# Token attention in the order differential, neighbourhood, plain; two modulation parts in every step from the first step on

## What is computed

```python
for l in range(2):
    mod_x = silu(c) @ w_ada[l] + b_ada[l]              # six vectors of 1024: shifts, scales, gates
    hx = modulate(rms_norm(x, g1), sh1, sc1)           # the same for ctx
    q.. k.. v.. = split(hx @ w_in[l])                  # for three mixers
    # a, plain: 8 heads of 64, 2 key heads, softmax over 512 + 256 keys
    # b, neighbourhood: 4 heads of 64, a window of tokens (by a bias) + 256 context keys
    # c, differential: 4 heads, each two softmaxes of 32-wide halves
    w  = p[:, :, 0] - lam * p[:, :, 1]
    oc = rms_norm(w @ v, g_sub) * (1 - lam_init)       # normed per head, 64 wide
    x = x + gate1 * (concat([oa, ob, oc]) @ w_out[l])
    x = x + gate2 * conv_ffn(modulate(rms_norm(x, g2), sh2, sc2))
# then the second block: two layers of mixer, memory attention and feed-forward
```

## Time and profile before

| | before |
|---|---|
| median of three runs | 3666.6 us (3666.44 to 3673.21) |
| the profiled execution | 3661.56 us, span 3659.7 us |
| PE busy | 3528.0 us (96%) |
| DVE busy | 1755.0 us (48%) |
| ACT busy | 1524.8 us (42%) |
| POOL busy | 1458.4 us (40%) |
| mean granted TensorE clock | 0.985 |
| chain that ended last | PE 89%, DVE 5%, ACT 3% |

### The profile page before, as it was taken

The page is one execution under the profiler, slowest core; times in us unless marked ns, Lnnn a source line. Parts: engine busy times, 40 slices in busy tenths (PEclk is TensorE's granted clock), DMA queues, the critical chain, the costliest instruction groups (busy, mean ns, idle before and its releaser), DMA issues.

```text
span 3659.7 us, 50085 instructions
## 1 busy us (share of the span) xinstructions
PE 3528.0 (96%) x19796; PEld 2799.3 (76%) x19796; DVE 1755.0 (48%) x2922; ACT 1524.8 (42%) x2557; POOL 1458.4 (40%) x986
## 2 busy tenths in 40 slices
PE   7999889999999999899999989999999989999998
PEld 5776567888899766578887768878887768888886
DVE  5766645423334766633542776161114686162114
ACT  4445554433455446534332355443223355443222
POOL 4520014444588510034444435344444444434442
PEclk8999999999999999999999999999999999999999
DMA  7613513333365411423333213223333213323331
GB/s 230 161 48 115 174 35 93 93 98 96 105 185 173 114 45 42 155 87 101 93 98 96 76 34 104 81 73 95 97 94 81 75 41 87 98 61 101 93 98 58
DMA packets 642466, 355.59 MB, mean 97 GB/s; under 512 B 70469, under 2 KB 614841, under 8 KB 642233
## 3 DMA queue, kind: packets, MB, share of 16 engines
q1 hardware_dynamic: 630379, 339.66, 32.2%
q10 hardware_dynamic: 11854, 12.72, 1.1%
HBM read 346.28 MB, written 6.05 MB: 96 GB/s over the span
## 4 chain that ended last, share of the span: by engine, by line
PE 89%; DVE 5%; ACT 3%; issue 2%; DMA 1%; POOL 1%; SPq 0%; ACTq 0%; DVEq 0%
PE psum L876 67%; PE psum L1105 5%; PE psum L1136 3%; PE psum L1156 2%; PE psum L900 1%; DVE neg_max L2013 1%; PE psum L1077 1%; ACT work L1574 1%; PE psum L980 1%; PE psum L904 1%; PE psum L1185 1%; PE psum L1036 1%; PE psum L931 1%; PE psum L1163 1%; PE psum L1015 1%
## 5 line engine op out<-in xcount | busy, mean ns | idle before, releaser
L859 POOL TENSOR_TENSOR w_lo<-w_raw,w_hi 128x256 fp32r<-128x256 f32 (+3 forms) x936 | 1396.5, 1512 | 2126.3 <-ACT w_hi L1413 2126.0
L876 PE MATMUL psum<-h_hi,w_hi 128*128 128x512 f32 (+1 forms) x2736 | 1034.2, 378 | 2.5 <-POOL w_lo L859 1.5
L876 PE MATMUL psum<-h_lo,w_hi 128*128 128x512 f32 (+1 forms) x2736 | 1010.1, 369 | 0.0
L876 PE MATMUL psum<-h_hi,w_lo 128*128 128x512 f32 (+1 forms) x2736 | 1010.1, 369 | 0.0
L1413 ACT ACTIVATE w_hi<-w_raw 128x1024 fp32r<-128x1024 f32 (+1 forms) x546 | 570.9, 1047 | 622.5 <-PE psum L876 587.6
L876 PEld LDWEIGHTS psum<-h_hi,w_hi 128*128 128x128 f32 x2736 | 516.5, 189 | 112.0 <-issue 19.8
L876 PEld LDWEIGHTS psum<-h_lo,w_hi 128*128 128x128 f32 x2736 | 516.5, 189 | 94.7 <-issue 9.9
L876 PEld LDWEIGHTS psum<-h_hi,w_lo 128*128 128x128 f32 x2736 | 516.2, 189 | 87.4
L876 PE MATMUL psum<-hid_hi,w_hi 128*128 128x512 f32 (+1 forms) x1040 | 393.0, 378 | 1.8 <-POOL w_lo L859 1.7
L876 PE MATMUL psum<-hid_lo,w_hi 128*128 128x512 f32 (+1 forms) x1040 | 391.8, 377 | 0.0
L876 PE MATMUL psum<-hid_hi,w_lo 128*128 128x512 f32 (+1 forms) x1040 | 391.8, 377 | 0.0
(11 more groups left out here) (248 smaller groups left out, 4280.1 us busy)
## 6 DMA issues: line engine op xcount, KB each, us to landing
w_raw<-in_w_up_dram SPq DMA_DIRECT2D x132, 512.0 KB, 3.8
w_raw<-in_w_ff_dram SPq DMA_DIRECT2D x128, 512.0 KB, 3.8
w_raw<-in_w_in_dram SPq DMA_DIRECT2D x92, 512.0 KB, 3.9
w_raw<-in_w_ada_dram SPq DMA_DIRECT2D x80, 512.0 KB, 4.2
w_raw<-in_w_down_dram SPq DMA_DIRECT2D x48, 512.0 KB, 3.6
w_raw<-in_w_mkv_dram SPq DMA_DIRECT2D x32, 512.0 KB, 3.9
w_raw<-in_w_down_dram SPq DMA_DIRECT2D x24, 384.0 KB, 3.1
w_ada_first<-in_w_ada_dram SPq DMA_DIRECT2D x4, 2048.0 KB, 18.0
```

The lines of the kernel that those rows point to most:

```text
L859: m = nc.gpsimd.tensor_tensor(WL[:, c % NSPLIT, k:k + step, :], RAW[:, c % NRAW, k:k + step, :], WH[:, c % NSPLIT, k:k + step, :].bitcast( ...
L876: m = pe.matmul(out_ap, lhs(a, k), rhs(b, k), start=(k == 0 and n == 0), stop=(k == nk - 1 and n == 2))
```

## The change

For the 512 tokens the plan is now built in the order differential (steps 0 to 15), neighbourhood (16 to 23), plain (24 to 39); the context attention keeps its order. Tiles and their numbers stay. The modulation parts are counted from step 0: steps 0 to 23 in layer 0, steps 0 to 15 in layer 1. The rest of the differential norm moves into the loop: one square root and one reciprocal for both groups at std_at = 19, and the spread of the two groups at i = 20 and 21. lam_ends moves to i = 0. A plain or neighbourhood group now waits for the low part of the last such group before it, where before it was simply the group before.

```diff
-ADA_LAST = 36
...
-    pair = step - ADA_LAST + len(parts) // 2
-    return parts[2 * pair:2 * pair + 2] if pair >= 0 else []
+    return parts[2 * step:2 * step + 2]
...
+            def plain():
+                for m in range(4):
...
+            def window():
+                for j in range(2):
...
+            def differential():
+                for j in range(2):
...
+            if stream == "x":
+                differential()
+                window()
+                plain()
+            else:
+                plain()
+                window()
+                differential()
...
+        def std_at(att):
+
+            return max(i for i, o in att["ends"].items() if att["groups"][o]["diff"] is not None) + 4 if att["wide"] else None
+
         def spread_at(att, i):
 
-            diff = [o for o, g in enumerate(att["groups"]) if g["diff"] is not None]
-            return [o for n, o in enumerate(diff) if i == len(att["steps"]) + 2 * n]
+            if att["wide"]:
+                return [o for n, o in enumerate(diff_groups(att)) if i == std_at(att) + 1 + n]
+            return [o for n, o in enumerate(diff_groups(att)) if i == len(att["steps"]) + 2 * n]
...
-                        pe.wait_ge(*at("sub_rstd", (S, o)))
+                        pe.wait_ge(*at("sub_rstd", S if att["wide"] else (S, o)))
...
-                    for o in spread_at(att, i):
+                    if att["wide"] and i == std_at(att):
+                        act.wait_ge(*at("sub_taken", (S, groups[diff_groups(att)[-1]]["bank"])))
+                        nc.scalar.activation(SUBS[:, :, :], SUBS[:, :, :], ACT.Sqrt, bias=EPSC[:, 0:1],
+                                             scale=1.0 / HEAD).then_inc(*mark("sub_std", S))
+                    for o in () if att["wide"] else spread_at(att, i):
...
-                    if S == ("att", "x", 0) and i == 2:
+                    if S == ("att", "x", 0) and i == 0:
                         lam_ends()
...
-                        if o and g["diff"] is None:
-                            dve.wait_ge(*at("o_lo", (S, o - 1)))
+                        if g["diff"] is None and plain_before(att, o) is not None:
+                            dve.wait_ge(*at("o_lo", (S, plain_before(att, o))))
...
+                    if att["wide"] and i == std_at(att):
+                        dve.wait_ge(*at("sub_std", S))
+                        nc.vector.reciprocal(SUBS[:, :, :], SUBS[:, :, :]).then_inc(*mark("sub_rstd", S))
                     for o in spread_at(att, i):
-                        dve.wait_ge(*at("sub_std", (S, o)))
-                        nc.vector.reciprocal(sub_stats(att, o), sub_stats(att, o)).then_inc(*mark("sub_rstd", (S, o)))
+                        if not att["wide"]:
+                            dve.wait_ge(*at("sub_std", (S, o)))
+                            nc.vector.reciprocal(sub_stats(att, o), sub_stats(att, o)).then_inc(*mark("sub_rstd", (S, o)))
```

More of the change, by code:

```diff
@@ L607, in values @@
                 return [[VN[:, j, col + 64 * lane:col + 64 * lane + 64] for j in vt] for lane in range(2)]
[L609 to L629, removed]
-                    turns.append(dict(parts=[(len(steps) - 2, 1), (len(steps) - 1, 1)], v=values(384 + 128 * j), t=t,
-                                      group=len(groups)))
-                groups.append(dict(tile=6 + j, diff=layer))
+            def plain():
+                for m in range(4):
+                    for t in range(nt):
+                        steps.append(dict(lanes=[rows(64 * lane, 64, m, 4, t) for lane in range(2)], nk=nk, adds=[[], []], mix=None))
+                        turns.append(dict(parts=[(len(steps) - 1, 0), (len(steps) - 1, 1)], v=values(0), t=t, group=len(groups)))
+                    groups.append(dict(tile=m, diff=None))
@@ new lines, in window @@
+            def window():
+                for j in range(2):
+                    for t in range(nt):
+                        adds = [[], []]
+                        if stream == "x":
+                            adds = [[(0, SEQ, TB[:, 2 * j + lane, 6 - 2 * t:14 - 2 * t, :].rearrange("p a b -> p (a b)"))]
+                                    for lane in range(2)]
+                        steps.append(dict(lanes=[rows(64 * lane, 64, 5 + j, 7 + j, t) for lane in range(2)], nk=nk, adds=adds,
+                                          mix=None))
+                        turns.append(dict(parts=[(len(steps) - 1, 0), (len(steps) - 1, 1)], v=values(P + 128 * j), t=t,
+                                          group=len(groups)))
+                    groups.append(dict(tile=4 + j, diff=None))
@@ new lines, in differential @@
+            def differential():
+                for j in range(2):
+                    for t in range(nt):
+                        for e in range(2):
+                            steps.append(dict(lanes=[rows(64 * e + 32 * m, 32, 9 + j, 11 + j, t) for m in range(2)], nk=nk,
+                                              adds=[[], []], mix=layer))
+                        turns.append(dict(parts=[(len(steps) - 2, 1), (len(steps) - 1, 1)], v=values(384 + 128 * j), t=t,
+                                          group=len(groups)))
+                    groups.append(dict(tile=6 + j, diff=layer))
```

5 lines of the change are left out of this document (added).

## The result

The changed kernel takes **3676.5 us** (median of 20 runs, 3663.8 to 3683.4) against 3666.6 for the kernel before (20 runs, 3662.5 to 3677.5): a ratio of 1.0019, with a 95% interval of 1.0011 to 1.0027. I had forecast 3656.7 and a range of 3650 to 3667. By the medians it is about 10 us slower where I expected 10 us less; by the ratio, which is estimated from all the runs and is not the quotient of the medians (that would be 1.0027), it is 7 us slower.

What follows compares the result with a forecast made beforehand. Dense PE products fill nearly all the span; only the two token attentions' loop periods were read. Terms: 1.2 + 1.1 - 6.8 - 5.4 = -9.9 us, giving 3651.7 for the profiled execution, 3656.7 for the median; range 3650 to 3667.

Steps and rivals of the forecast that it cites:

- Plain: Steps 24 to 39, fifteen intervals: 73.8 us in layer 0, 72.9 in layer 1.
- The norm: Root and spreads in neighbourhood steps 19 to 22: costs 3.8 us a layer, bounds 1.5 and 8.
- The mask: DVE's additions ahead of the maximum at i = 4 to 7: 2.0 us in a layer, between 0 and 4.3.
- the forecast's own pairs: Differential steps 0 to 15 with parts: eight pairs of steps at 10.05 us, 80.4 us.
- The two tails: Behind each token attention's last step: gain 6.8 us in layer 1, 5.4 in layer 0.
- The second handover: Second differential group, handed over in neighbourhood steps: 0.8 us, bounds 0 and 6.3, sums hidden behind DVE's adds.
- sign of being wrong: One of three stated signs: the handover in neighbourhood steps costs over 3 us.
- The first handover: First differential group, inside steps 0 to 15: 5.6 us extra, the mean of 4.9 to 6.3 from the earlier profile.
- The start: First differential steps, where nothing is in flight: 0.7 us.
- Rival (a): Loop takes the gain back: second handover 5.6, or norm at its upper end; 3664.6 us, no change; chance 0.18.
- Rival (c): Slower: PE's clock falls at stops at i = 10, 18, 21; one layer +4.8, both +19, 3686 us; chance 0.08.
- the one on table loads: Trainium skill rule: 1283 ns a load, about 1380 ns drain; the prediction saw no drain behind the load.

Runs made afterwards that it cites:

- run 4: Changed kernel with the window mask added to the bias tables by GpSimd instead of DVE in steps 4 to 7: 3671.0 us, 0.9998 of the kernel before.
- Run 5: Changed kernel with DVE taking the sums of squares out of PSUM between the two lanes, not behind both lanes' additions and maxima: 3668.1 us, ratio 0.9995.
- busy start: Run numbered 9: changed kernel with four unread matmuls behind step 0's scores and two behind step 1's, in both token attentions: 3667.8 us, ratio 0.9996.
- run 11: Kernel before, old order and parts, with the mask on GpSimd and the busy start: 3668.5 us, 0.9997 of the kernel before.
- run 7: Changed kernel with six unread matmuls ahead of PE's wait for the square at each handover: 3667.9 us, 1.0002 of the kernel before.
- run 3: Changed kernel with the differential norm's root, reciprocal and spreads six steps later, in plain steps 25 to 27: 3673.9 us, ratio 1.0012.
- helps: Three edits to the changed kernel: late sums, mask on GpSimd, busy start. All together: 3660.4 us, 0.9974 of the kernel before.
- late sums: Changed kernel with PE making the sums of squares at the end of step e + 3, DVE taking them at e + 4's start: 3662.8 us, ratio 0.9989.
- run 8: Changed kernel with the late sums and the mask on GpSimd together: 3659.7 us, 0.9974 of the kernel before.

## Why the prediction was wrong

**The method stood: the period of the loop, by kind of step.** Plain 73.9 and 72.9 (forecast 73.8, 72.9). The norm 2.4 to 2.9, counted with 3.8. The mask 1.4 a layer by run 4, and 2.1 and 2.4 over the forecast's own pairs, counted with 2.0. The two tails, read by setting each ACT instruction of before beside the same one of after: after is 17.4 us late at layer 1's last exponential and 10.1 at 1592 us of before, a gain of 7.3, counted with 6.8. In layer 0 it is 12.5 late at the last exponential and 6.6 at the second context scores, a gain of 5.9, counted with 5.4; of this 1.6 is lost again by 490 us.

**The second handover, 0.8 counted, cost 4.2 us in layer 0 and 3.0 in layer 1** (the interval ahead of step 19 is 10.8 and 9.0 us, in before it was 6.6 and 6.0). This is the step that failed: I argued that "the adds make DVE late anyway and the sums of squares hide behind them". The sums did hide. What I didn't follow was their bank: who empties it, and what that engine has ahead of the emptying. DVE's queue was the very reason I gave for the cover, and it was the wait. Run 5 took back 3.2 a layer by moving 0.15 us of work. The prediction's sign of being wrong, that this handover "costs over 3", showed in layer 0 and stood at its edge in layer 1. Another 2.4 us in layer 1, the interval from step 16 to 17 at 9.0 (6.6 before, with no parts there), wasn't in the sum either. It is the stop of 2.47 us shown above, at DVE's queue again; it stayed at 8.6 to 10.7 with the sums moved, the longer ones with more time at 1.2 GHz behind the stop (3.4 us at 8.6, 10.2 at 10.7). No run takes it away.

**The first handover, 5.6 counted, cost 9.6 in layer 0 and 4.9 in layer 1** (29.7 and 25.0 for what 20.1 would do). The stop was the 1.39 us of the earlier trace rows both times. The difference between the layers goes with the clock: 0.53 in the window behind the stop in layer 0, and a single short stretch in layer 1. I had averaged two handovers of before, where the same difference had already shown itself (26.4 us with 6.8 at 1.2 GHz, 25.0 with 3.4), and read it as a spread of one price.

**The start, 0.7 counted, cost 1.9 in each layer.** Four intervals took 22.9 and 22.8, where two pairs of 10.05 would take 20.1, and the first of the mask's additions is 0.9 of the difference: without the mask on DVE (run 4) they take 22.0 in both layers. A busy start, with the mask, takes 20.4. The low clock behind step 0 was there before, too, but for 3.4 us instead of 10.2, though PE stood still for 2.95 us there. In differential steps with nothing in flight PE waits twice for exponentials before it has transposes to do (PE, layer 0 of after):

```profile
246.57 2.36 PE L1129 MATMUL psum<-qk_t 32*128 32x512 f32 x8 [2.19 <-ACT work L1598]
...
251.95 2.93 PE L1129 MATMUL psum<-qk_t 32*128 32x512 f32 x8 [1.20 <-ACT work L1598]
```

This is the size of a term that I gave without any row. The last four intervals before step 16, at 22.2 and 21.7 us, were 2.1 and 1.6 over two pairs as well; the sum had nothing for them, and what they are made of stays open.

**The rivals (a) and (c) were each right in part.** Rival (a) priced the second handover at 5.6 instead of 0.8; it measured 4.2 and 3.0, and the time that it gave, 3664.6, is 12 us short. Rival (c), to which I gave 0.08, had the mechanism, a clock that falls at new stops. It priced one layer at +4.8 over before and both at +19; the medians are 9.9 apart and the profiles 14.8. The square of the first group was a right place. At i = 18 the low clock came, but behind the bank and not the square, for which PE didn't wait; at DVE's queue at i = 21 no low clock shows. The start and layer 1's step 16 were not among its places. Its argument against, that window and plain steps keep PE almost full, held for plain steps only.

**The rest of the 14.8.** Exponential 0 of layer 0 came 1.2 later than in before; in the kernels with the new order it starts anywhere from 243.0 to 244.7. Another 2.2 arose outside the loops and their tails, 1.4 between the two attentions (from 8.2 late at 490 us to 9.6 at layer 1's first exponential) and 0.8 behind the second, and 4.1 us arose at 2165, in the second block, where both kernels run the same instructions. PE there, of before and then of after, 10.88 us later:

```profile
2154.46 0.63 PE L1136 MATMUL psum<-const_sb,work 128*128 128x128 f32 x4 [0.88 <-ACT work L1574]
```
```profile
2165.34 0.97 PE L1160 MATMUL psum<-const_sb,work 128*128 128x128 f32 x4 [0.88 <-ACT work L1598]
```

The same matmuls, with the same 0.88 us of idle time before them and the same offsets up to this row; in one execution the clock falls here, in the other it doesn't. The window 2160 to 2180 has 1.00 in before and 0.83 in after. Of the thirteen kernels that were profiled after the one before, six others lost 4.0 to 4.1 us here too, run 11 with the old order among them, four lost 1.6 and two nothing. So it isn't the change's, and a single pair of profiles can be off by so much. From the -9.9 of the forecast to the 14.8 of the profiles it is 24.7 us: 16.8 in the loops, 1.0 less for the tails as they were counted, 1.6 just behind the first of them, and 1.2, 2.2 and 4.1 in the places above, to within 0.2.

The Trainium skill, "TensorE: Matmul & The Clock Gate", section "HAM oscillation — how this bites in real kernels", prices the low clock at the time spent in it times (1 - 1.2/2.4). Here 145.8 - 115.0 = 30.8 us more at 1.2 GHz would be 15.4 us, and the profiles are 14.8 apart. The two numbers agree, but partly by luck, since shorter tails and longer stops stand in the 14.8 as well: run 7 has 101.5 us at 1.2 GHz, less than before, and is still 3.1 us **over** it in its profile. The same page, section "A second HAM failure mode: psum-queue depth-cycling", tells of a clock that swings where PE idles often and briefly between groups of matmuls that cycle through PSUM; the start, the handovers and the stretch at 2165 look like that (idle times of 0.3 to 2.2 us), and it would have been the rule to weigh against this change in place of the one on table loads, for moving the norm with its loads (run 3) left the long interval as it was.

## What to carry to other kernels

When an instruction of 0.15 us empties a buffer that another engine's next step needs, its place in the queue is worth more than its length: ask of every PSUM bank in a rotation what its emptier has ahead of it. Where a change puts stops of a microsecond into a stretch in which PE was kept going, count each with the clock that may fall behind it, and let filler work stand in it when the stop can't go. Take differences of a few us from several timed runs; the profiles then say only where they arose.

## What the runs showed of the hardware

- **Idle matmuls pay.** Six matmuls that nobody reads, 2.86 us of PE on the path at each handover, make the kernel 6.2 us faster (run 7, uncertain by 4.3), and in the window behind the first handover of layer 0 the granted clock is 1.00 instead of 0.53.
- **The helps don't seem to add.** 11.0, 7.7 and 8.4 us alone, 16.5 together, a difference only just clear of noise. The late sums and the mask by themselves do add (18.7 us alone, 16.5 together in run 8, equal within the noise); the busy start brings nothing on top of them.
- **A stop has no fixed price.** The stop of 1.39 us at the first handover was followed by 13.7 us at 1.2 GHz in layer 0 and by 3.4 in layer 1 of the same execution. It isn't shown to be mere chance: runs 3, 5 and 9, which leave this stop as it is, have 13.7 in layer 0, too, and 3.4 to 6.8 in layer 1, while run 4 has 6.8 and 10.2. The same instructions at 2165 kept or lost the clock. Over the 20 runs of after the time and the mean granted clock go together with a correlation of -0.97, from 3663.8 us at 0.985 to 3683.4 at 0.978. Nearly the whole spread of this kernel's runs goes with its clock.
- **Removing work from PE can gain nothing.** In the old order's layer 0 the differential steps take 83.3 us with modulation parts in 12 of them and 83.6 us without: at a clock of 0.96 with them, 0.75 without. In the new order's layer 0, though, steps 0 to 16 got 8.9 us shorter without theirs.
